# RWKV-7 block inverse on one TensorE: the two heads' left-hand products of the first doubling issued together, one head evacuated in two half copies

## The reference, cut to what matters

```python
def step(S, inp):
    r_t, w_t, k_t, v_t, kk_t, a_t = inp
    s_kk = jnp.einsum('...vk,...k->...v', S, kk_t)
    S = (S * w_t[..., None, :] - s_kk[..., :, None] * (kk_t * a_t)[..., None, :]
         + v_t[..., :, None] * k_t[..., None, :])
    return S, jnp.einsum('...vk,...k->...v', S, r_t)
```

## Time and profile before

| | |
|---|---|
| median of 3 runs | 3713.86 us (3713.68 to 3714.92) |
| span of the profiled execution | 3711.9 us |
| PE busy | 3456.7 us, 93% |
| DVE busy | 1631.2 us, 44% |
| ACT busy | 1048.9 us, 28% |
| POOL busy | 677.6 us, 18% |
| mean granted TensorE clock | 0.978 |
| the eight turns of layer 0 | from about 901 to 1520 us |
| the eight turns of layer 1 | from about 2705 to 3268 us |

### The profile page before, as it was taken

The page is one execution under the profiler, slowest core; times in us unless marked ns, Lnnn a source line. Parts: engine busy times, 40 slices in busy tenths (PEclk is TensorE's granted clock), DMA queues, the critical chain, the costliest instruction groups (busy, mean ns, idle before and its releaser), DMA issues. The chain is left out here.

```text
span 3711.9 us, 92740 instructions
## 1 busy us (share of the span) xinstructions
PE 3456.7 (93%) x41758; PEld 1938.9 (52%) x41758; DVE 1631.2 (44%) x2896; ACT 1048.9 (28%) x1844; POOL 677.6 (18%) x583
## 2 busy tenths in 40 slices
PE   6989999999999999999999597998999999999997
PEld 3454444545666666443332345656656666774333
DVE  3584803664766663221000356824256666531111
ACT  2211002504545543111111321104145555420001
POOL 0151200302434332010000002113033333300000
PEclk8999999999999999999999799999999999999998
DMA  5103622341110111359998211833311111268996
GB/s 203 64 5 108 221 68 80 120 136 41 27 36 23 28 34 48 115 205 421 404 393 343 101 46 46 260 113 103 93 27 36 26 31 31 53 225 369 424 424 272
DMA packets 255517, 538.69 MB, mean 145 GB/s; under 512 B 49520, under 2 KB 173696, under 8 KB 222224
## 3 DMA queue, kind: packets, MB, share of 16 engines
q1 hardware_dynamic: 236064, 463.98, 34.3%
q0 software_dynamic: 19056, 68.69, 5.3%
HBM read 514.75 MB, written 17.87 MB: 143 GB/s over the span
## 5 line engine op out<-in xcount | busy, mean ns | idle before, releaser
L1299 PE MATMUL banks<-sb_h,sb_ring 128*128 128x512 f32 (+1 forms) x1344 | 476.4, 513 | 10.1 <-DMA sb_ring<-w_branch 6.5
L1816 PEld LDWEIGHTS banks<-inv 64*64 64x64 f32 x15104 | 290.3, 134 | 170.6 <-issue 168.4
L1299 PEld LDWEIGHTS banks<-sb_h,sb_ring 128*128 128x128 f32 x1344 | 255.5, 191 | 224.0 <-issue 196.6
L1816 PE MATMUL banks<-inv 64*64 64x64 f32 x15104 | 328.5, 221 | 14.3 <-issue 10.6
L1825 PE MATMUL banks<-sb_h,sb_ring 128*128 128x512 f32 (+1 forms) x672 | 329.6, 598 | 6.2 <-DMA sb_ring<-w_in 4.1
L819 PE MATMUL banks<-sb_h,sb_ring 128*128 128x512 f32 x512 | 232.1, 611 | 19.4 <-SPq L241 19.4
L3189 PE MATMUL banks<-gu,xs 128*64 128x512 f32 x768 | 169.5, 594 | 5.1 <-DMA gu<-gu_pairs 4.6
L819 PEld LDWEIGHTS banks<-sb_h,sb_ring 128*128 128x128 f32 x512 | 99.8, 197 | 138.8 <-issue 118.1
L2533 DVE COPY inv<-banks 128x512 f32<-128x512 f32 x144 | 98.9, 691 | 164.9 <-PE banks L1816 164.1
L3341 DVE TENSOR_TENSOR hrow<-hrow,banks 128x256 f32<-128x256 f32 x36 | 15.1, 421 | 355.2 <-ACT hrow L3377 355.2
L1299 PE MATMUL banks<-sb_branch,sb_ring 128*128 128x512 f32 (+1 forms) x512 | 170.9, 487 | 0.0
(11 more groups left out here) (484 smaller groups left out, 5663.8 us busy)
## 6 DMA issues: line engine op xcount, KB each, us to landing
gu<-gu_pairs SPq DMA_DIRECT2D x64, 1536.0 KB, 16.8
gu<-gu_tiles SPq DMA_DIRECT2D x57, 1024.0 KB, 8.4
sb_ring<-w_in SPq DMA_DIRECT2D x24, 2048.0 KB, 9.3
sb_ring<-gu_tiles SPq DMA_DIRECT2D x39, 1024.0 KB, 9.2
vtok<-w_mod POOLq DMA_DIRECT2D x64, 512.0 KB, 5.5
sb_ring<-down_pairs SPq DMA_DIRECT2D x32, 1024.0 KB, 14.7
sb_ring<-w_in SPq DMA_DIRECT2D x58, 512.0 KB, 3.9
sb_ring<-down_tiles SPq DMA_DIRECT2D x25, 1024.0 KB, 8.4
```

What stands on the lines that cost most here:

```text
L1299: mm = nc.tensor.matmul(out, left(kt), right(kt), start=kt == 0, stop=kt == KT - 1)
L1816: m = mm(k.bank[bank][H[to], at:at + w], left, right, start=start, stop=True, skip_group_check=True)
```

## The change

In stage 5 the second and the third step become one. Before, head 0's product into XT (16 matmuls, cross 0) and head 1's (16 matmuls, cross 0) follow each other, each on the same two quarters. Now both stand in one step, and head 1's has cross 1, so that its results land in the other half of the PSUM bank. Head 1's evacuation puts them back: instead of one copy of 128x512 there are two copies of 64x512, from half q into half q ^ 1, each counted on the same semaphore. Nothing else is moved; ACT, POOL and SP have the same instructions in the same order.

```diff
@@ STAGES
     [[(0, "q1", "n0", "n1", 0, "copy", 1), (1, "q1", "n0", "n1", 1, "copy", 3)],
-     [(0, "n0", "q1", "XT", 0, "vcopy", 2)],
-     [(1, "n0", "q1", "XT", 0, "vcopy", 6)]],
+     [(0, "n0", "q1", "XT", 0, "vcopy", 2), (1, "n0", "q1", "XT", 1, "vswap", 6)]],
@@ stage_counts
-                v += how != "copy"
+                v += (how != "copy") + (how == "vswap")
@@ rwkv_heads, DVE's inverse
                     dst, src = slot(h, into), eight(k.bank[bank])
-                    if how == "vcopy":
+                    if how == "vswap":
+                        for q in range(2):
+                            nc.vector.tensor_copy(dst[H[q ^ 1]], src[H[q]]).then_inc(s.ev_v, 1)
+                    elif how == "vcopy":
                         nc.vector.tensor_copy(dst, src).then_inc(s.ev_v, 1)
```

## The result

The changed kernel takes 3720.64 us (median of 18 runs) against 3712.12 us before (18 runs on the same chip): ratio 1.0025, 95% interval 1.0017 to 1.0034, some 8.5 us slower by the medians (9.3 by the ratio). The forecast was +4.1 us. The time lies inside the range, the direction is right, and the size is half of what was measured. The profiled execution's span grew from 3711.9 to 3722.6 us, by 10.7. The 18 runs of the change spread from 3709.26 to 3733.57 us, so one profile shows one of several outcomes.

The account below looks back on a forecast made before the run. PE and DVE were taken to end together, within 0.05 us, ahead of stage 6. Layer 1 +4.4, layer 0 0, its last turn -0.25 give +4.1 us on the 3711.9 span, 3716.0; runs 1.96 above: 3718.0 us, range 3712.5 to 3722.0.

Parts of the forecast that it names:

- What bounds: Start of stage 6: PE's filler ends and DVE's copy frees PE within 0.05 us, so stage 6 waits for both.
- Part 1, PE: Stage 5 on PE: filler starts 2.03 us after stage 5's first weight load (A), not 2.94; 0.91 us gained per turn.
- Part 2, DVE: DVE copies after stage 5: three in a row, half copies 0.68 us each, so stage 6 starts 0.55 us late.
- the middle row: Middle of three copy spacings after stage 5: one after the other at 0.04 us, third copy ending at A+4.33.
- Part 3, layer 0 covered: Layer 0, seven turns: DVE waits for POOL masks anyway, so stage 6's 0.55 us delay costs 0.
- if layer 0's turns get longer: One of the signs named beforehand that would show the forecast wrong; layer 0's seven turns were forecast to lose 0.
- The last turn: Layer 0's last turn, with a longer filler and no features on DVE: stage 6 starts 0.25 us earlier.
- Part 3, layer 1 pays 8 x 0.55 = 4.4 us: Layer 1, eight turns: what follows hangs on PE and stage 6's start, so each 0.55 us delay passes on.
- So the clock is no part of this case.: Opening reading of one turn per layer: PE at full granted clock of 1.00, so no clock cost was priced.
- Rival 6 (issue waits move): PE waits that the profile puts down to issue, 16.4 us in 30 places, move and carry it out of range; chance 0.05.
- The bound: Whole kernel: a difference under 0.2% (7.4 us) was held indistinguishable from no change; chance of slower than that 0.14.
- Rival 3: Layer 0's first L2454 behind the copies comes after mask 1's end, cover breaks: about +8 us, 3722; chance 0.10.

Follow-up runs that it names:

- e2_same_quarters: Changed kernel, but head 1 with cross 0 on the same two quarters and one whole copy: 3720.33 us, ratio 1.0010 to the kernel before.
- e1_again: The changed kernel run once more without edit, for a second profile: 3726.47 us, ratio 1.0031 to the kernel before.
- e8: Changed kernel, stage 6 not waiting for DVE's XT copies and DVE's feature work moved behind the inverse's copies: ratio 0.9975 to the kernel before.
- e9: Changed kernel, stage 6 not waiting for DVE's XT copies, stage 7 waiting for them instead: ratio 0.9998 to the kernel before.
- e4: Changed kernel with two projection matmuls behind stage 5 and one behind stage 6, not one and two: 3721.77 us, ratio 1.0018 to before.

## Why the prediction was half right, step by step

- **What bounds (balanced to 0.05 us, PE and DVE).** Right: stage 6 starts 0.27 behind the end of DVE's last copy, as before, in 31 of the 32 turns that the two profiles of the change show.
- **Part 1, PE: filler at A+2.03, 0.91 us gained.** Right: A+2.02 to A+2.05 in half of the change's turns; short issue waits make it A+2.18 in the turn shown above, long ones up to A+3.72. The gain was not usable, as forecast.
- **Part 2, DVE: half copies at 0.68 each, stage 6 0.55 late.** Right. Half copies took 0.68 and 0.69, stage 6 started at A+4.55 to A+4.71 in the turns without a long issue wait, forecast A+4.60. The gaps were 0.03, the middle row: a half copy starts 0.03 behind the end of the copy ahead, where two whole copies overlap and take 1.29 together in e2_same_quarters. The Trainium skill ("VectorE: DVE Perf Modes", section "Two Vector instructions with no wait between them") has the rule that an instruction which changes its start quadrant, a group of 32 partitions, is held until all earlier ones have finished. The trace agrees with it.
- **Part 3, layer 0 covered.** Right in six of the seven turns it was claimed for: `apply_inverse` at A+10.49 to A+10.51 in all but the fifth. The fifth met an issue wait of 1.20 us in stage 5 (0.78 before), fell to the lower clock and lost 3.15 us; in e1_again it kept the clock, met a wait of 1.75 and started `apply_inverse` at A+11.63. So the cover held against the copies, not against the waits, and by the prediction's own sign ("if layer 0's turns get longer") one turn of seven went wrong. The last turn gained 0.21, forecast 0.25.
- **Part 3, layer 1 pays 8 x 0.55 = 4.4 us.** Right as far as it goes: 4.6 us in e2_same_quarters, which has this delay without the long idle time. The two profiles of before lie 2.3 us apart here, so the agreement is no closer than that.
- **The step that failed** is in the first paragraph: "So the clock is no part of this case." It was read from two turns of the kernel before, where PE idled 0.04 us in this place. Even that kernel loses the clock in a turn that was not read: in the fifth of layer 0, behind an issue wait of 2.90 us, it is 0.50 from 1263.8 on. The change itself opened 1.4 us of idle time ("PE idles from A+3.09 to A+4.60") and I priced that at its delay alone. The lower clock level then cost about 1.5 us in each turn of layer 1 that it met, 3.0 us in either profile. In the first profile the fifth turn of layer 0 lost 3.15 us besides, 2.6 of it between stages 6 and 7 (5.65 in place of 3.04). For layer 1 the account closes roughly: against the mean of the two profiles of before (79.46 us) the change takes 8.6 us more and e1_again 9.3, where 4.4 of forecast delay, 3.0 of clock and 1.6 and 2.0 of longer issue waits make 9.0 and 9.4. For the whole program it stays open: 4.1 + 6.1 = 10.2 and 4.1 + 3.0 = 7.1, where the runs give 8.5 and 11.4, and one profile does not say how many turns fall in the other executions.
- **Rival 6 (issue waits move)** was half seen. They stand at the same counts of instructions, as expected, and their sum moved by no more than it does from run to run (19.9 and 20.0 us in the change's profiles, 16.4 and 21.7 before). But where they fell into stage 5 the idle time came on top, and the clock fell in 5 of 12 such turns. No rival named that.
- **The bound** of 0.2% was crossed by the ratio, though its interval begins at 0.17%; so the outcome is slower, to which I gave 0.14. Rival 3, which I had made responsible for most of that, did not occur: L2453 came 0.24 us ahead of the first mask's end.
- **Luck.** The range held by luck: its upper end was set by rival 3, which did not occur, and the median beside the change was 3712.12, 1.74 us below the 3713.86 that the forecast started from. 8.5 us on 3713.86 would have been 3722.4, outside.

## What to carry to other kernels

Where two engines end together, speed on the one that does not end last turns into idle time, and here idle time on TensorE had its own price, about 1.5 us for each turn of layer 1 in which the clock fell: put other matmuls there (a filler moved forward kept the clock in the one profile taken) or take away the wait. A copy that was split by partitions cost as much per piece as the whole (0.68 to 0.69 against 0.69 us); ask first whether the next stage needs it at all, since here the wait could be put off by a stage and the feature work put behind the copies, which gained 0.26% with or without the merged step.

## What the runs showed of the hardware that was not expected

- TensorE fell to its lower level after 0.7 to 1.4 us of idle time behind the copies with an issue wait of 1.0 to 2.4 us shortly before, in 5 of 32 turns of the change; after 2.6 us without a filler in 14 of 16; after an issue wait of 1.84 or 2.11 us alone in one turn each of e8 and e9, though other waits of 1.8 us and more left the clock as it was; in e2 and e4, where the idle time behind the copies was some 0.5 us in most turns and the issue waits up to 1.84 us, in none.
- At the lower level 64 weight loads of stage 6 took 1.83 us in place of 1.05, and in layer 1 stage 7 began 4.5 us behind stage 6 in place of 3.03.
- Two half copies that change their partitions' half do not overlap (1.41 us together), two whole ones do (1.29 us).
- With the merged step and the late wait PE met more issue waits in layer 1's eight stretches, 10.0 us on average against 6.1 without the step, in overlapping groups of four and five profiles.
